# TensorE's order inside the attention loops: transposes of a pair ahead of the product with V

## The chip, the cores and the metric

One Trainium2 chip, one core. The metric is the device time of the whole program in microseconds (us). The engines are TensorE (PE; its weight loads are shown apart as PEld), VectorE (DVE), ScalarE (ACT), GpSimd (POOL) and SyncE (SP).

## What is computed

Two models of depth two run one after the other on 256 tokens of width 1024. The second also carries 256 context tokens in its first layer. Most of the time goes to plain products with streamed weights. The change touches only the three attention loops:

```python
# first model, layer 1 ("nsa"): 16 heads, 256 queries; p over 256 keys for two branches (selected, window), plus a compressed branch
s = einsum(qc, k) - slope * distance ;  p = masked_softmax(s) ;  o = einsum(p, v)
# second model, layer 0 (512 tokens) and layer 1 (256 latent queries, 512 keys)
"gqa": s = einsum(q, k) ;          p = softmax(s) ; o = einsum(p, v)
"na":  s = einsum(q, k) + bias ;   p = softmax(s) ; o = einsum(p, v)
```

The output is the normalised state of the 256 tokens.

## The kernel before, in words

The program is written engine by engine; each engine runs its own list in order and waits on semaphores where it needs another's result. The order of work around the change is written out by hand in four functions of the same name, `softmax`, one each for PE (L717), ACT (L1143) and DVE (L1507), over the list that `attention_jobs` (L243) gives. No planner sets it.

A job is one head and 128 queries. Jobs go in pairs (two heads that share the rows of a tile), numbered u = 0, 1, 2 and so on. The first loop, called **nsa** here, has 16 pairs; even pairs have q = 0 (128 keys in each of two branches) and odd pairs q = 1 (256 keys in each). The second loop, **layer 0**, has 32 pairs, 16 of kind gqa and then 16 of kind na; within each kind u mod 4 is 0 or 1 for queries over 512 keys and 2 or 3 for queries over 256 keys. The third loop, **layer 1**, has 16 pairs, 8 gqa and then 8 na, all over 512 keys.

What is done to pair u, step by step:

- PE computes the **scores** of both heads into a double bank of PSUM (L734 to L740; two double banks, `score_pairs`), and waits first for ACT's exponentials of pair u-2 in that bank (L727). Its matmuls are recorded by the helper `mm`, L579.
- DVE adds the causal term (L1524, nsa) or the position bias (L1531, na, 256 of its keys), and takes the row **maximum** (L1535; for gqa a factor at L1538).
- ACT takes the **exponentials** into `s_p`, one of four buffers per head (L1166), recorded at L1020, with the row sums read by an extra instruction each.
- DVE takes the reciprocal of the sums (L1545; L1550 multiplies the gates in, nsa) and scales the rows: the **normalisation** (L1555), which signals `prob_ready`. DVE does this for pair v-1 after the maximum of pair v.
- PE makes the **transposes** (L781) into `turn_pair`, banks 6 and 7 of PSUM, of which there is one copy: 8 matmuls of 128x128 in most pairs, 4 where the pair has half the keys. They wait for `prob_ready` of the pair and for ACT's copy of pair u-1, and signal `turned_full`.
- ACT **copies** the transposed rows to SBUF (L1156), into one half of a buffer `pT` that holds two pairs, and signals `turned_ready`.
- PE makes the **product with V** of two pairs at once, in every even turn, and signals `o_full`; ACT copies its result out (L1174).

PE's loop runs over turns v. Turn v has the scores of pair v; in even turns from v = 4 the product with V of pairs v-4 and v-3; and from v = 2 the transposes of pair v-2. In ACT's loop, turn v has the copy of pair v-2, then the exponentials of pair v, and in odd turns the copy of a product.

Two waits in an even turn v matter. The product with V waits for `turned_ready` of pair v-3, and so do the transposes of pair v-2 (both ask for v-2 copies in the loop). And ACT's copy of pair v-2 overwrites the half of `pT` from which the product of this same turn reads pair v-4; it waits for it:

```python
act.wait_ge(turned_full, base // 2 + u + 1)                    # L1152
if u >= 2:
    act.wait_ge(o_full, base // 4 + (u - 2) // 2 + 1)          # L1154
```

For even u = v-2 that is the product of turn v; for odd u it is the product of the turn before.

Of the kernel before, what the change touches and what calls it, by code (L numbers as in the profile page):

```python
# [31 lines left out]
P = 128  # L32
# [237 lines left out]
def turned_blocks(kind, q):  # L270

    if kind == "nsa":
        return [2 * br + b for br in range(2) for b in range(q + 1)]
    return list(range(len(key_blocks(kind, q))))
# [14 lines left out]
def program(nc, wstream, params_in, consts_in, rpb_in, c_in, x_in, out):  # L289
    ctx = ExitStack()  # L290
    with ctx:
# [280 lines left out]
        def _(pe):  # L572
# [144 lines left out]
            def softmax(layer=None):  # L717

                jobs = attention_jobs(layer)
                pairs = len(jobs) // 2  # L720
                base = jobs_done.base
                for v in range(pairs + 3):
                    if v < pairs:
                        kind, t, _, q = jobs[2 * v]
                        qs = slice(q * P, (q + 1) * P)
                        if v >= 2:
                            pe.wait_ge(prob_exp, base + 2 * v - 2)  # L727
                        for p in range(2):
                            rows_ = slice(DH * p, DH * p + DH)
                            bank = score_pairs[v % 2][:, p, :]  # L730
                            if kind == "nsa":

                                nk = (q + 1) * P
                                ins = mm(bank.rearrange("p (b k) -> p b k", b=2)[:, :, 0:nk], n_q[rows_, t, qs],  # L734
                                         n_k[rows_, :, t // GROUP, 0:nk], start=True, stop=True)
                            else:
                                a = 0 if q < 2 else S
                                key = a_nak[rows_, t, a:S2] if kind == "na" else a_gk[rows_, a:S2]
                                qq = (a_naq if kind == "na" else a_gq)[rows_, t, qs]
                                ins = mm(bank[:, 0:S2 - a], qq, key, start=True, stop=True)  # L740
                        ins.then_inc(score_full, 1)
                    if v >= 4 and v % 2 == 0:

                        i = 2 * (v - 4)
                        kind, t, _, q = jobs[i]
                        out_ = (base + i) // 4
                        if out_ >= 2:
                            pe.wait_ge(o_free, out_ - 1)
                        pe.wait_ge(turned_ready, (base + i) // 2 + 2)
                        pT = n_pT if kind == "nsa" else a_pT  # L750
                        terms = []
                        for p in range(2):
                            head = head_of(kind, t, p)
                            if kind == "nsa":
                                g = head // GROUP
                                mine = [(n_vz[:, head, :], n_pcT[:, :, g, :], 0)]
                                for b in range(2):
                                    for br in range(2):
                                        k = (br * 2 + b) * P
                                        mine.append((n_v[:, b, (br * KV + g) * DH:(br * KV + g + 1) * DH], pT[:, 2 * b + p::2, k:k + P], b))  # L760
                            else:
                                mine = []
                                for n, b in enumerate(key_blocks(kind, q)):
                                    val = a_nav[:, b, head * DH:(head + 1) * DH] if kind == "na" else a_gv[:, b, p * DH:(p + 1) * DH]
                                    mine.append((val, pT[:, p::2, n * P:(n + 1) * P], 0))
                            terms.append(mine)
                        last = len(terms[0]) - 1
                        for n in range(last + 1):
                            for p in range(2):
                                val, pr, first = terms[p][n]  # L770
                                ins = mm(out_banks[out_ % 2][DH * p:DH * p + DH, first * P:S], val, pr, start=n == 0, stop=n == last)
                        ins.then_inc(o_full, 1)
                    if 2 <= v < pairs + 2:
                        u = v - 2
                        kind, t, _, q = jobs[2 * u]
                        pe.wait_ge(prob_ready, base + 2 * u + 2)
                        if u >= 1:
                            pe.wait_ge(turned_ready, base // 2 + u)
                        for p in range(2):
                            for b in turned_blocks(kind, q):  # L780
                                ins = nc.tensor.transpose(turn_pair[:, p, b * P:(b + 1) * P], s_p[:, (2 * u + p) % 4, b * P:(b + 1) * P], ident)  # L781
                        ins.then_inc(turned_full, 1)
                jobs_done.base += len(jobs)

            pe.wait_ge(ones_ready, 1)
# [1187 lines left out]
```

## Time and profile before

| | before |
|---|---|
| median of 3 runs | 2247.96 us (2245.68 to 2248.45) |
| profiled execution, its own time | 2248.55 us |
| its span | 2246.7 us |
| PE busy | 2103.2 us (94%) |
| DVE busy | 1514.9 us (67%) |
| ACT busy | 875.6 us (39%) |
| granted TensorE clock, mean | 0.97 |

In the rows below times are in us from the start of the span. A matmul's end is modelled, so that successive groups of matmuls overlap by some hundredths; the distance from start to start is what counts. A granted clock of 1.00 is TensorE at 2.4 GHz and 0.50 is 1.2 GHz. In square brackets stands how long the engine was idle before the row, and which engine's instruction ended that.

### The profile page before, as it was taken

Reading aid. Unit: us, or ns where it says so; the run is one execution under the profiler, and the core shown is the slowest. Engines: PE = TensorE matmul, PEld = TensorE weight load, DVE = VectorE, ACT = ScalarE, POOL = GpSimd, SP = SyncE. Lnnn points to the kernel's source line nnn. Section 1 sums busy time; section 2 is a strip of 40 time slices with the busy share of each in tenths; the row PEclk is TensorE's granted clock in tenths of the full one; section 3 lists DMA queues with packets and bytes.
Section 4 is the critical chain, followed back from the end, with each engine's and each line's share of the span. In section 5 each row is a group of like instructions: output and inputs, shape, how many; then the busy total and the mean of one; then the engine's idle time right before and its main releaser. Section 6 shows DMA issues by size and latency. Waiting matters only on the chain.

```text
span 2246.7 us, 33659 instructions
## 1 busy us (share of the span) xinstructions
PE 2103.2 (94%) x12858; PEld 1791.8 (80%) x12858; DVE 1514.9 (67%) x2859; ACT 875.6 (39%) x1376; POOL 249.5 (11%) x231
## 2 busy tenths in 40 slices
PE   7899999879999799889899989999997998999998
PEld 6789999748999588646567568888886865998998
DVE  7658898395888669776698863383276966355554
ACT  4634444273444432475211242212214336435443
POOL 0003321003330010000000002201211000001220
PEclk9999999889999899999999999999998999999999
DMA  6345465404556322103455422252243310344552
GB/s 234 121 175 190 179 248 209 149 1 165 188 179 260 134 95 76 57 1 132 152 213 207 170 111 94 93 193 107 94 169 123 131 57 20 151 176 162 186 187 78
DMA packets 46987, 318.09 MB, mean 142 GB/s; under 512 B 5008, under 2 KB 8080, under 8 KB 9488
## 3 DMA queue, kind: packets, MB, share of 16 engines
q1 hardware_dynamic: 45568, 309.58, 37.4%
q0 software_dynamic: 1296, 6.82, 0.8%
q8 instruction: 84, 1.38, 0.2%
q14 instruction: 39, 0.32, 0.0%
HBM read 315.33 MB, written 1.05 MB: 141 GB/s over the span
## 4 chain that ended last, share of the span: by engine, by line
PE 72%; DVE 17%; ACT 5%; issue 3%; DMA 2%; DVEq 0%; ACTq 0%; SPq 0%
PE ps L579 68%; DVE ps L1373 4%; DVE w_lo L1353 4%; ACT arena L1020 3%; DMA ring<-wstream 2%; PE ps L781 2%; PE ps L627 1%; DVE arena L1337 1%; DVE small L1535 1%; DVE rs L1319 1%; DVE arena L1555 1%; DVE h_lo L1347 1%; ACT w_hi L1020 1%; ACT L1020 1%; DVE ps L1524 1%
## 5 line engine op out<-in xcount | busy, mean ns | idle before, releaser
L579 PE MATMUL ps<-h_hi,w_hi 128*128 128x256 f32 (+1 forms) x2616 | 849.2, 325 | 48.7 <-DVE h_lo L1347 30.7
L579 PE MATMUL ps<-h_lo,w_hi 128*128 128x256 f32 (+1 forms) x2616 | 834.9, 319 | 0.0
L579 PE MATMUL ps<-h_hi,w_lo 128*128 128x256 f32 (+1 forms) x2616 | 833.8, 319 | 0.0
L1353 DVE TENSOR_TENSOR w_lo<-ring,w_hi 128x1024 fp32r<-128x1024 f32 x433 | 545.2, 1267 | 356.5 <-ACT w_hi L1020 355.7
L1020 ACT ACTIVATE w_hi<-ring 128x1024 fp32r<-128x1024 f32 x433 | 452.3, 1055 | 582.0 <-PE ps L579 476.6
L579 PEld LDWEIGHTS ps<-h_hi,w_hi 128*128 128x128 f32 x2616 | 503.0, 192 | 98.7 <-issue 42.9
L579 PEld LDWEIGHTS ps<-h_lo,w_hi 128*128 128x128 f32 x2616 | 504.6, 193 | 33.2 <-issue 1.2
L579 PEld LDWEIGHTS ps<-h_hi,w_lo 128*128 128x128 f32 x2616 | 504.5, 193 | 33.0
L1020 ACT ACTIVATE arena<-ps 128x512 f32<-128x512 f32 (+2 forms) x246 | 140.9, 575 | 461.1 <-PE ps L579 415.1
L1373 DVE SCALAR_TENSOR_TENSOR ps<-ring,arena 128x512 f32<-128x512 f32 x384 | 250.8, 725 | 0.0
L579 PE MATMUL ps<-arena,ring 128*128 128x256 f32 (+2 forms) x840 | 217.6, 420 | 20.6 <-DMA ring<-wstream 7.8
L579 PE MATMUL ps<-hid_hi,w_hi 128*128 128x256 f32 (+1 forms) x736 | 224.6, 305 | 0.9 <-DVE w_lo L1353 0.9
L579 PE MATMUL ps<-hid_lo,w_hi 128*128 128x256 f32 (+1 forms) x736 | 224.3, 305 | 0.0
L579 PE MATMUL ps<-hid_hi,w_lo 128*128 128x256 f32 (+1 forms) x736 | 224.3, 305 | 0.0
L579 PEld LDWEIGHTS ps<-arena,ring 128*128 128x128 f32 x840 | 150.9, 193 | 84.2 <-issue 54.5
L520 POOL CAST hid_hi<-arena 128x256 f32 (+3 forms) x92 | 82.5, 897 | 1024.8 <-DVE arena L1471 1024.8
L579 PE MATMUL ps<-arena 128*64 128x256 f32 (+4 forms) x800 | 129.5, 449 | 28.4 <-ACT arena L1020 24.7
L579 PEld LDWEIGHTS ps<-hid_hi,w_hi 128*128 128x128 f32 x736 | 138.4, 188 | 9.4 <-issue 1.2
L579 PEld LDWEIGHTS ps<-hid_lo,w_hi 128*128 128x128 f32 x736 | 138.1, 188 | 8.2
L579 PEld LDWEIGHTS ps<-hid_hi,w_lo 128*128 128x128 f32 x736 | 138.0, 188 | 8.1
L1687 DVE SCALAR_TENSOR_TENSOR arena<-arena,prm 128x512 f32<-128x512 f32 (+1 forms) x240 | 129.9, 613 | 0.4
L579 PEld LDWEIGHTS ps<-arena 128*64 128x64 f32 (+1 forms) x800 | 63.4, 174 | 70.4 <-issue 37.4
(153 smaller groups left out, 1673.3 us busy)
## 6 DMA issues: line engine op xcount, KB each, us to landing
ring<-wstream SPq DMA_DIRECT2D x290, 1024.0 KB, 4.8
arena<-c_in POOLq DMA_DIRECT2D x7, 512.0 KB, 4.5
arena<-rpb POOLq DMA_DIRECT2D x2, 1536.0 KB, 8.2
x<-x_in SPq DMA_DIRECT2D x2, 1024.0 KB, 12.1
out<-arena SPq DMA_DIRECT2D x8, 128.0 KB, 2.0
cst<-consts SPq DMA_DIRECT2D x1, 928.0 KB, 11.9
prm<-params SPq DMA_DIRECT2D x1, 580.0 KB, 10.6
ring<-wstream SPq DMA_DIRECT2D x1, 512.0 KB, 3.5
```

What stands on the lines that cost most here:

```text
L520: nc.gpsimd.tensor_copy(hi, products[:, e, 0:N]).then_inc(pool_step, 1)
L579: ins = nc.tensor.matmul(*a, **k)
L627: ins = nc.tensor.matmul(psO[:, 0:N], ones[:], sq[:, k % 4, 0:N], start=k == 0, stop=k == KD - 1)
L781: ins = nc.tensor.transpose(turn_pair[:, p, b * P:(b + 1) * P], s_p[:, (2 * u + p) % 4, b * P:(b + 1) * P], ident)
L1020: return nc.scalar.activation(o, i, f, **k)
L1319: link(V.reciprocal(rs[:, 0:N], rs[:, 0:N]))
L1337: V.scalar_tensor_tensor(out=scaled[:, n % 8, :], in0=x[:, k, c], scalar=gain(k, s), in1=rs[:, c], op0=ALU.mult, op1=ALU.mult).then_inc(sc ...
L1347: ins = V.scalar_tensor_tensor(out=h_lo[:, k, c], in0=t, scalar=bias(k, s), in1=hi, op0=ALU.add, op1=ALU.subtract)
L1353: V.tensor_tensor(w_lo[:, job % SPLITS, :], raw_job(job), w_hi[:, job % SPLITS, :].bitcast(F32), ALU.subtract).then_inc(weights_ready, 1)
L1373: V.scalar_tensor_tensor(out=ps[4 + p][:], in0=w, scalar=1.0, in1=c[s][:, p * S2:(p + 1) * S2], op0=ALU.mult, op1=ALU.mult, accum_out=mod_ ...
L1524: ins = V.scalar_tensor_tensor(out=sc, in0=c, scalar=slope, in1=sc, op0=ALU.mult, op1=ALU.add)
L1687: return V.scalar_tensor_tensor(out=cy[:, c, 0:ns, :], in0=a_u3[:, c, 0:ns, bass.ds(j, S)], scalar=w, in1=cy[:, c, 0:ns, :], op0=ALU.mult, ...
```

## The change

In PE's loop the block that makes the transposes of pair v-2 stands ahead of the block that makes the product with V, where it stood behind it. Both blocks keep their instructions, waits and signals. Nothing else changes; odd turns have no product with V, and turns 2 and 3 and those from pairs + 2 on have only one of the two blocks, so the order of their work is the same.

```diff
                         ins.then_inc(score_full, 1)
+                    if 2 <= v < pairs + 2:
+                        u = v - 2
+                        kind, t, _, q = jobs[2 * u]
+                        pe.wait_ge(prob_ready, base + 2 * u + 2)
+                        if u >= 1:
+                            pe.wait_ge(turned_ready, base // 2 + u)
+                        for p in range(2):
+                            for b in turned_blocks(kind, q):
+                                ins = nc.tensor.transpose(turn_pair[:, p, b * P:(b + 1) * P], s_p[:, (2 * u + p) % 4, b * P:(b + 1) * P], ident)
+                        ins.then_inc(turned_full, 1)
                     if v >= 4 and v % 2 == 0:
...
                         ins.then_inc(o_full, 1)
-                    if 2 <= v < pairs + 2:
-                        u = v - 2
-                        kind, t, _, q = jobs[2 * u]
-                        pe.wait_ge(prob_ready, base + 2 * u + 2)
-                        if u >= 1:
-                            pe.wait_ge(turned_ready, base // 2 + u)
-                        for p in range(2):
-                            for b in turned_blocks(kind, q):
-                                ins = nc.tensor.transpose(turn_pair[:, p, b * P:(b + 1) * P], s_p[:, (2 * u + p) % 4, b * P:(b + 1) * P], ident)
-                        ins.then_inc(turned_full, 1)
                 jobs_done.base += len(jobs)
```

## Rows read from the trace of the kernel before

**Rows 1.** The page, busy time, share of the span and instructions of PE.
```profile
PE 2103.2 (94%) x12858; PEld 1791.8 (80%) x12858; DVE 1514.9 (67%) x2859; ACT 875.6 (39%) x1376; POOL 249.5 (11%) x231
```
**Rows 2.** Busy time by stretch, the three loops: PE, PEld, DVE, ACT, POOL, PEclk, DMA.
```profile
449.00:511.00 62.00, 48.73 (x320) 29.52 (x320) 51.35 (x145) 41.90 (x152) 0.00 (x0) 0.86 0.00 1
932.00:1030.00 98.00, 80.68 (x514) 46.44 (x515) 65.92 (x160) 71.26 (x179) 0.15 (x1) 0.97 0.00 1
1839.00:1900.00 61.00, 50.80 (x320) 28.33 (x320) 42.36 (x88) 42.06 (x89) 0.00 (x0) 0.97 0.00 1
```
**Rows 3.** Chain of waits and list of waits (total, times, longest), 445 to 511 us.
```profile
by line: DVE arena L1555 21.4%; DVE ps L1524 21.3%; DVE small L1535 21.1%; PE ps L579 12.9%; ACT arena L1020 5.1%; DVE small L1550 3.7%; PE ps L781 3.4%; PE ps L893 3.0%; issue 2.4%; DVE small L1545 2.2%; DVE arena L1636 1.1%; DVE arena L16
...
PE ps L781 <- DVE arena L1555: 5.6, 7, 1.2
```
**Rows 4.** Timeline of the nsa loop, turn 10 and the start of turn 11.
```profile
479.13 1.29 DVE L1524 SCALAR_TENSOR_TENSOR ps<-cst,ps 128x512 f32<-128x512 f32 x2
480.29 0.70 PE L579 MATMUL ps<-arena 64*128 64x256 f32 x4
480.40 1.02 ACT L1020 ACTIVATE arena<-ps 128x1024 f32<-128x1024 f32 x1 [0.76 <-PE ps L781]
481.57 1.95 PE L579 MATMUL ps<-arena 128*64 128x256 f32 x20 [0.57 <-ACT arena L1020]
481.99 0.87 DVE L1555 TENSOR_SCALAR arena<-arena,small 128x128 f32<-128x128 f32 x4
483.45 0.65 PE L781 MATMUL ps<-cst,arena 128*128 128x128 f32 x4
484.04 1.13 PE L579 MATMUL ps<-arena 64*128 64x512 f32 x4
485.63 1.29 DVE L1524 SCALAR_TENSOR_TENSOR ps<-cst,ps 128x512 f32<-128x512 f32 x2
```
**Rows 5.** Timeline of the nsa loop, turns 16 to 18.
```profile
501.51 0.88 DVE L1555 TENSOR_SCALAR arena<-arena,small 128x128 f32<-128x128 f32 x4
...
504.80 1.09 PE L781 MATMUL ps<-cst,arena 128*128 128x128 f32 x8 [1.18 <-DVE arena L1555]
507.09 3.50 PE L579 MATMUL ps<-arena 128*64 128x256 f32 x20 [1.21 <-ACT arena L1020]
```
**Rows 6.** Timeline of layer 0, kind gqa: turn 12 (first row) and turn 14.
```profile
966.17 0.62 DVE L1555 TENSOR_SCALAR arena<-arena,small 128x256 f32<-128x256 f32 x2
...
972.43 0.88 DVE L1555 TENSOR_SCALAR arena<-arena,small 128x512 f32<-128x512 f32 x2
...
973.65 1.09 PE L781 MATMUL ps<-cst,arena 128*128 128x128 f32 x8
```
**Rows 7.** Timeline of layer 0, kind na: turn 22.
```profile
995.27 0.88 DVE L1555 TENSOR_SCALAR arena<-arena,small 128x512 f32<-128x512 f32 x2
...
996.21 1.09 PE L781 MATMUL ps<-cst,arena 128*128 128x128 f32 x8 [0.43 <-DVE arena L1555]
```
**Rows 8.** Timeline of layer 1: turn 6 (gqa), turn 10 (na).
```profile
1857.76 3.01 PE L579 MATMUL ps<-arena 64*128 64x512 f32 x20 [0.36 <-ACT arena L1020]
1857.94 0.88 DVE L1555 TENSOR_SCALAR arena<-arena,small 128x512 f32<-128x512 f32 x2
...
1870.91 3.01 PE L579 MATMUL ps<-arena 64*128 64x512 f32 x20 [0.18 <-ACT arena L1020]
1871.69 0.88 DVE L1555 TENSOR_SCALAR arena<-arena,small 128x512 f32<-128x512 f32 x2
...
1873.85 1.09 PE L781 MATMUL ps<-cst,arena 128*128 128x128 f32 x8
1874.87 1.13 PE L579 MATMUL ps<-arena 64*128 64x512 f32 x4
```
**Rows 9.** Busy time by stretch, as rows 2: ends of nsa and of layer 1.
```profile
503.40:506.90 3.50, 1.31 (x11) 0.86 (x8) 1.30 (x5) 1.60 (x4) 0.00 (x0) 1.00 0.00 0
...
1893.20:1897.80 4.60, 2.21 (x18) 1.72 (x17) 0.49 (x2) 2.17 (x3) 0.00 (x0) 1.00 0.00 0
```

## The prediction, made before the changed kernel ran

> **What bounds the kernel now.** The page first: PE is busy for 94% of the span, so that most of the program is a stream of matmuls the change does not touch [rows 1]. The stretches of the three attention loops come next [rows 2]. They are different: the nsa loop has PE busy for 48.7 of 62 us and DVE for 51.4, layer 0 has PE 80.7 of 98 and layer 1 50.8 of 61. No engine is full in any of them for the whole stretch, hence the time is set by a cycle of waits that goes round once in two turns, and I read that cycle from the timelines. DMA moves nothing in them (share 0.00), and the weights' queue on SP waits for no instruction that is moved, so no transfer enters the argument. What follows a loop is bound by PE and can only start when the loop has ended; a loop that ends later moves all that follows by as much.
>
> In nsa the chain goes for over 60% through DVE's L1555, L1524 and L1535, one after another, and PE waited 7 times for the normalisation before transposes, 5.6 us in all [rows 3]. In turn 10 PE makes the scores from 480.29, waits 0.57 us for ACT's copy of pair 7 (begun at 480.40), runs 20 matmuls of the product from 481.57, transposes from 483.45, and has turn 11's scores from 484.04 [rows 4]. Put simply, in an even turn the product waits for the copy, and the transposes for the copy and the normalisation. The normalisation of turn 10 began at 481.99 and took 0.87: it ended at 482.86, under the product. That is the cover which the change takes away.
>
> **The change, part by part.** No instruction is added or removed, nothing goes to another engine, no DMA is moved. In each even turn that has both blocks two things change.
>
> (a) The transposes now stand directly behind the scores. They cannot start before the normalisation, so PE idles where it ran the product. Behind the waiting transposes are queued the product and then the next turn's scores.
>
> (b) ACT's copy of the transposed rows can't profit. It waits for the product of the same turn too (L1154), since it overwrites what that product reads. Today it starts when transposes end; afterwards it starts when the product ends. Call T the moment at which both blocks of an even turn are done. Today and afterwards the copy and the next scores start from T. So the price of the change is how much later T is, turn by turn, if everything else keeps its distance from T.
>
> The steps, from rows. The hand-over from DVE's end to PE's transposes is 0.06 (996.21 less 995.27 and 0.88) [rows 7]. Four transposes advance PE by 0.59 (484.04 less 483.45) [rows 4], eight by 1.02 (1874.87 less 1873.85) [rows 8]. The product advances it by 1.88 in nsa (483.45 less 481.57) [rows 4]. In layer 1 scores and product together take 2.94 (1873.85 less 1870.91), of which the scores are some 1.08 and the product 1.86 [rows 8].
>
> *nsa, 7 turns (4 to 16).* New T in turn 10, with the normalisation's end where it is: 482.86 + 0.06 + 0.59 + 1.88 = 485.39, against 484.04 today, 1.35 later [rows 4]. DVE's next step on those scores, the bias add, starts at the earliest 1.17 behind T (1.13 of scores and a hand-over): 486.56. Today DVE starts it at 485.63, 1.59 behind T, since it is busy until then. So 0.42 of the 1.35 disappears in that slack, and 0.93 per two turns is left. The new cycle closes: bias add to the end of the normalisation is 482.86 less 479.13, or 3.73; 3.73 + 2.53 + 1.17 = 7.43 against 6.50 (485.63 less 479.13). Six such turns make 5.6 us. In the seventh, turn 16, the normalisation ends at 501.51 + 0.88 = 502.39, the product at 504.92, the copy follows by 0.10 and the last transposes follow the start of that copy (half the size of the one of 1.02 us, 0.60) by some 0.74; they start at 505.76, against 504.80 today [rows 5]: 0.96. Together 6.5 us.
>
> *Layer 0, 15 turns (4 to 32).* In 8 of them (v a multiple of 4) the pair to be transposed has half the keys, and its normalisation is done at 966.17 + 0.62 = 966.79, before the scores of that turn, which began at 965.99 and last over 1 us, are finished [rows 6]. The copy ends last there for both blocks and the swap costs nothing; what hides the swap is the copy, and if that were 0.3 us shorter, nothing would be lost either. In 3 gqa turns (6, 10, 14) the normalisation ends at 972.43 + 0.88 = 973.31. Transposes at 973.37, eight of them to 974.39, and then the product. It has 8 matmuls, half of those that take 1.86 in layer 1 [rows 8], so 0.93 and a hand-over, say 1.0: T is 975.39 against 973.65 + 1.02 = 974.67 today, 0.7 each [rows 6]. In 4 na turns (18, 22, 26, 30) PE already waits 0.43 for DVE behind the product, so the whole product of 1.0 comes on top [rows 7]. There DVE's chain hangs on T of the turn before and moves with it. Sum 3 x 0.7 + 4 x 1.0 = 6.1 us.
>
> *Layer 1, 7 turns (4 to 16).* In the 3 gqa turns the normalisation ends at 1858.82, and PE, with the scores done at 1858.84, would start at 1858.88: 0.04 each [rows 8]. In na DVE has the bias add in front of its maximum, so the normalisation is later: 1871.69 + 0.88 = 1872.57. Transposes from 1872.63 to 1873.65, product to 1875.51, against 1874.87: 0.64 [rows 8]. Turn 16 is taken like it. Sum 0.1 + 4 x 0.64 = 2.7 us.
>
> **Sum:** 6.5 + 6.1 + 2.7 = 15.3 us, onto the profiled execution's 2248.55: 2263.9, rounded to 2264. The median of the runs stands 0.6 below that execution, so by the median it would be 2263.3. Outside the loops I cost the edit at nothing. Waits that PE has in odd turns (for ACT's copy, and in nsa for DVE, 5.6 us in 7 times [rows 3]) all hang on T or get shorter, since DVE gains time there; nothing in rows lets them grow.
>
> **Unknown costs, from both sides.** The clock is the one thing that rows of today do not show for the new pattern. From 503.40 to 506.90 PE was busy for 1.31 of 3.50 us, in waits of 1.18 and 1.21, and then the product ran at 3.50 instead of 1.95: the granted clock had fallen from 2.4 to 1.2 GHz [rows 4, 5, 9]. At layer 1's end PE was busy for 2.21 of 4.60 us and the clock stayed at 1.00 [rows 9]. The new nsa turns have one idle stretch of about 2 us, longer than these waits, but with PE busier on either side. (From the scores' end, 480.99, to 482.92 it is 1.9 with today's times [rows 4]; normalisation moves 0.9 away, and the rest is a matter of how far the odd turn's wait for DVE, some 0.8 [rows 3], shrinks.) A fall costs, for as long as it lasts, 1.55 on a product (3.50 for 1.95) and in the same ratio 0.5 on four transposes and 0.9 on the scores that DVE waits for, 3 us per two turns. Lower end nothing, upper end all seven nsa turns, 21 us. I take nothing, by the nearest row: the new turns have one long wait each and a product and scores on either side, like layer 1's end, which kept the clock, where nsa's end had two waits with only transposes between. A gain is not excluded: a product which starts right behind transposes has its weights loaded already, and no wait of its own to come back from. That hand-over is 0.15 at most (481.57 less 480.40 and 1.02) [rows 4].
>
> **Rivals.**
>
> *The clock falls in nsa, and perhaps in layer 0's na turns.* For it: nsa's end today [rows 5, 9]. Against it: layer 1's end [rows 9]. Two of the nsa turns at half clock give 6 us more, 2270; all seven 2285. I give this rival 0.22. The Trainium skill (TensorE: Matmul & The Clock Gate, Part 4: PE-mode transpose) says transposes don't count as work for the clock in the way matmuls do. By that rule the new order invites the fall, since it puts transposes right behind the idle stretch, and the time would be this rival's 2270 and not 2264. The trace agrees at nsa's end, where between the products of turns 16 and 18 only transposes ran and the clock fell [rows 5, 9]; at layer 1's end the stretch that holds the transposes of turns 16 and 17 left it up [rows 9], so the trace does not decide.
>
> *DVE draws level.* If the normalisation, freed of other lateness, came 0.4 us sooner in nsa and na turns than the fixed distance from T, each of 14 turns would lose less: about 8 to 10 us in all, 2257. For it: DVE has idle time in layer 0 (65.9 of 98). Against: what it waits for there are scores, which follow T. 0.10.
>
> *Not slower: one wait instead of two.* If the normalisation reached PE before the copy in every even turn, as it does in 8 of the 29, the swap would cost nothing and save one hand-over of up to 0.15 per turn, 29 x 0.15 = 4 us: 2244. It decides at the end of the even turn's scores; the normalisation stands 0.04 to 2 us behind that point in 21 turns [rows 4, 6, 7, 8]. 0.05.
>
> *The change doesn't do what it says.* PE's list is executed in the order written and no other engine's list sets the order of the two blocks; 2248, 0.02.
>
> **How the numbers follow.** Forecast 0.61, clock 0.22, DVE 0.10, not slower 0.05, no change 0.02. A difference of 0.2%, 4.5 us, is about what a measurement of this kernel can tell from none. Slower by over 0.2% holds the first three, 0.93; within it 0.04; faster 0.03. The range reaches down to 2257, the DVE case, and up to 2271, two or so turns at half clock. The predicted time is the sum, 2264.
>
> **What would show it.** Right: in the nsa loop pairs of turns 7.4 us apart instead of 6.5, transposes of even turns idle before them until DVE's L1555, the product directly behind, ACT's copy behind the product; layer 0's na turns 1.0 longer, layer 1's gqa turns unchanged. Wrong: even turns of the old length, or a copy by ACT that starts before the product has ended, or a granted clock of 0.50 inside a loop beyond its first turns.

## The result, and the profile of the changed kernel

The changed kernel took 2275.12 us (median of 4 runs, 2274.14 to 2275.74) against 2248.2 (median of 4, 2245.68 to 2250.75) for the kernel before: a ratio of 1.0119, 95% interval 1.0102 to 1.0137. It is slower, as forecast, but by 27 us where 15 were forecast, and outside the range of 2257 to 2271. The profiled execution took 2274.14 us, its span is 2272.3; against the profiled execution of before that is 25.6 us more.

The first part of the page of the changed kernel: busy time, share and instructions. The work is the same, count for count [rows 1]. PE is busy for 9.5 us longer, its weight loads for 3.1, and the other engines for 0.3 at most; as PE makes the same matmuls, some of them must have run slower.

```profile
PE 2112.7 (93%) x12858; PEld 1794.9 (79%) x12858; DVE 1515.2 (67%) x2859; ACT 875.6 (39%) x1376; POOL 249.5 (11%) x231
```

To see where the 25.6 us are I cut both timelines at the first scores matmul of each loop and at the first matmul behind it, and at the last matmul of the program (9.2 us follow it in both), in us:

| stretch | before | changed | difference |
|---|---|---|---|
| up to nsa | 449.55 | 452.57 | 3.0 |
| nsa loop | 61.52 | 71.11 | 9.6 |
| nsa to layer 0 | 421.36 | 420.07 | -1.3 |
| layer 0 loop | 97.17 | 106.42 | 9.25 |
| layer 0 to layer 1 | 809.43 | 808.89 | -0.5 |
| layer 1 loop | 61.21 | 66.80 | 5.6 |
| from there to the last matmul | 337.29 | 337.26 | 0.0 |

24.4 us are in the three loops, 1.2 outside them. The stretches outside vary from execution to execution of any kernel here: the one up to nsa has lain between 449.6 and 453.9, the one up to layer 1 between 805.5 and 813.8. In the loops the price was forecast as 6.5, 6.1 and 2.7.

The timeline of the nsa loop of the changed kernel, PE alone, from turn 6 on (x24 is the product and the next turn's scores in one row):

```profile
473.78 0.66 PE L750 MATMUL ps<-cst,arena 128*128 128x128 f32 x4 [2.06 <-DVE arena L1555]
474.36 4.69 PE L579 MATMUL ps<-arena 128*64 128x256 f32 x24
...
482.90 0.66 PE L750 MATMUL ps<-cst,arena 128*128 128x128 f32 x4 [2.05 <-DVE arena L1555]
483.49 3.01 PE L579 MATMUL ps<-arena 128*64 128x256 f32 x24
486.43 1.09 PE L750 MATMUL ps<-cst,arena 128*128 128x128 f32 x8
...
490.35 0.66 PE L750 MATMUL ps<-cst,arena 128*128 128x128 f32 x4 [2.05 <-DVE arena L1555]
490.93 4.65 PE L579 MATMUL ps<-arena 128*64 128x256 f32 x24
```

Two things are to be seen. First the pattern: an even turn's transposes wait some 2.05 us for the normalisation, the product stands directly behind, and from 482.90 to 490.35 two turns take 7.45 us, where they took 6.50 and were forecast at 7.43 [rows 4]. Second, two rows that break it: the same 24 matmuls take 4.69 and 4.65 us instead of 3.01, and those pairs of turns take 9.12 and 9.08. The views of the same stretch for DVE and ACT show where T's delay goes:

```profile
480.11 1.02 ACT L1020 ACTIVATE arena<-ps 128x1024 f32<-128x1024 f32 x1
...
481.97 0.87 DVE L1555 TENSOR_SCALAR arena<-arena,small 128x128 f32<-128x128 f32 x4
...
485.55 0.60 ACT L1020 ACTIVATE arena<-ps 128x512 f32<-128x512 f32 x1 [1.65 <-PE ps L579]
...
486.55 1.29 DVE L1524 SCALAR_TENSOR_TENSOR ps<-cst,ps 128x512 f32<-128x512 f32 x2 [0.85 <-PE ps L579]
```

ACT's copy (485.55) waits for the product, DVE's bias add (486.55) for the scores behind it, 0.85 us idle: DVE, which was the chain in this loop [rows 3], now stands still for PE. The list of waits of the changed kernel, 445 to 517 us (total, times, longest), has them beside PE's:

```profile
PE ps L750 <- DVE arena L1555: 15.8, 8, 2.8
...
DVE ps L1524 <- PE ps L579: 10.3, 9, 2.5
```

The timeline of layer 0, kind na, PE: turns 22 and 26. The wait is 1.38 us where it was 0.43 [rows 7]; in the second pair the product of 12 matmuls takes 2.93 instead of 1.72.

```profile
1011.09 1.09 PE L750 MATMUL ps<-cst,arena 128*128 128x128 f32 x8 [1.38 <-DVE arena L1555]
1012.11 1.72 PE L579 MATMUL ps<-arena 128*64 128x256 f32 x12
...
1023.42 1.46 PE L750 MATMUL ps<-cst,arena 128*128 128x128 f32 x8 [1.38 <-DVE arena L1555]
1024.81 2.93 PE L579 MATMUL ps<-arena 128*64 128x256 f32 x12
```

The timeline of layer 1's end, PE: an na turn, turn 16, and the last two products.

```profile
1901.06 1.09 PE L750 MATMUL ps<-cst,arena 128*128 128x128 f32 x8 [0.53 <-DVE arena L1555]
...
1915.34 1.09 PE L750 MATMUL ps<-cst,arena 128*128 128x128 f32 x8 [1.84 <-DVE arena L1555]
1916.37 1.95 PE L579 MATMUL ps<-arena 128*64 128x256 f32 x16
...
1921.86 3.53 PE L579 MATMUL ps<-arena 128*64 128x256 f32 x16 [1.21 <-ACT arena L1020]
```

What the slow rows have in common is in the busy time by stretch of the changed kernel (columns as in rows 2; the third from the end is the granted clock):

```profile
474.50:477.90 3.40, 3.40 (x20) 1.96 (x18) 2.00 (x7) 0.26 (x1) 0.00 (x0) 0.51 0.00 0
491.50:494.90 3.40, 3.40 (x20) 1.97 (x18) 1.58 (x7) 0.71 (x2) 0.00 (x0) 0.50 0.00 0
1024.00:1027.40 3.40, 3.40 (x17) 1.76 (x15) 0.94 (x3) 0.63 (x2) 0.00 (x0) 0.50 0.00 0
1037.60:1041.00 3.40, 3.40 (x17) 1.69 (x15) 0.93 (x3) 0.69 (x2) 0.00 (x0) 0.51 0.00 0
1921.70:1925.10 3.40, 3.24 (x16) 1.91 (x16) 0.00 (x0) 0.29 (x2) 0.00 (x0) 0.50 0.02 5
```

Five stretches at 1.2 GHz, each just behind a wait of PE for DVE or ACT, in places where the kernel before had 2.4. They cost 1.65 us each in nsa (9.12 or 9.08 less 7.45), some 1.25 each in layer 0 (the first 13.59, from 1023.42 to 1037.01, less 12.33, from 1011.09), and 1.6 in layer 1 (3.53 less 1.95): 7.4 us. A fall in nsa's last turns stands in both kernels (3.4 us from 506.9 before, from 515.4 now) and cancels.

One more difference of the clock is easily missed, in the first turns of layer 1. The scores of turn 3, PE's timeline, before (first row) and in the changed kernel:

```profile
1848.39 1.13 PE L579 MATMUL ps<-arena 64*128 64x512 f32 x4
1868.62 2.04 PE L579 MATMUL ps<-arena 64*128 64x512 f32 x4
```

Half clock lasted 3.4 us there before (from 1844.9) and 6.8 now (from 1863.7). It is not the swap's doing alone, if at all: e2 and e8 below keep layer 1's old order and have the 6.8 too, and turn 5's transposes begin 17.96 and 17.81 us into their loop, against 17.30 before and 18.36 in the changed kernel. So some 0.6 us of layer 1's 5.6 belong to that stretch.

Of the 24.4 us all this leaves 6.3 (nsa), 6.7 (layer 0) and 3.4 (layer 1), 16.4 in all, for waits, and 8.0 for the clock.

### The profile page after: what moved, and what is told of

The parts are those of the page before. It is cut to its first block, busy times and chain, and to the rows that moved or that the text cites. A ratio compares the mean times of both kernels' runs of the same rounds, so it can differ in the third digit from the quotient of the medians.

```text
span 2272.3 us, 33659 instructions
## 1 busy us (share of the span) xinstructions
PE 2112.7 (93%) x12858; PEld 1794.9 (79%) x12858; DVE 1515.2 (67%) x2859; ACT 875.6 (39%) x1376; POOL 249.5 (11%) x231
## 3 DMA queue, kind: packets, MB, share of 16 engines
q8 instruction: 84, 1.38, 0.2%
HBM read 315.33 MB, written 1.05 MB: 139 GB/s over the span
## 4 chain that ended last, share of the span: by engine, by line
PE 73%; DVE 18%; ACT 4%; issue 3%; DMA 2%; DVEq 0%; ACTq 0%; SPq 0%
PE ps L579 69%; DVE ps L1373 4%; DVE w_lo L1353 4%; DMA ring<-wstream 2%; ACT arena L1020 2%; PE ps L750 2%; PE ps L627 1%; DVE small L1535 1%; DVE arena L1337 1%; DVE rs L1319 1%; DVE arena L1555 1%; DVE h_lo L1347 1%; ACT w_hi L1020 1%; ACT L1020 1%; DVE arena L1687 1%
## 5 line engine op out<-in xcount | busy, mean ns | idle before, releaser
L579 PE MATMUL ps<-arena 128*64 128x256 f32 (+4 forms) x800 | 136.3, 473 | 21.4 <-ACT arena L1020 18.4
L522 POOL TENSOR_TENSOR hid_lo<-arena,hid_hi 128x256 f32 (+3 forms) x92 | 114.9, 1249 | 15.1 <-POOL hid_hi L520 14.8
```

What stands on the lines that cost most here:

```text
L522: nc.gpsimd.tensor_tensor(lo, products[:, e, 0:N], hi.bitcast(F32), ALU.subtract).then_inc(pool_written, 1)
L579: ins = nc.tensor.matmul(*a, **k)
```

## The experiments

The theory: 16 to 17 us are waits (the queue on PE holds the product and the next scores behind the normalisation), and some 7 us the clock, which falls because of them. The rivals: the copy by ACT, which now waits for its own turn's product, is the price; the clock is noise that comes and goes without the change; the cost is in the swap itself and is the same in every turn. All kernels but two (e9, e10) compute all of the reference. `product_of` and `turn_of` are the two blocks of the diff, as functions; "before" and "changed" say which order the turns not named have.

**e1, e2, e3: the swap in one loop at a time.**

```diff
-                    product_of(v)
-                    turn_of(v)
+                    if layer is None:        # e1; layer == 0 in e2, layer == 1 in e3
+                        turn_of(v)
+                        product_of(v)
+                    else:
+                        product_of(v)
+                        turn_of(v)
```

> Transposes first in the nsa loop only. Theory (PE idles for the normalisation, 0.93 us a pair of turns, and the longer idle stretches make the granted clock fall, some 1.6 us a time): 6.5 us of waits and about 3 of clock, so 9 to 10 us slower than before; pairs of turns 7.4 apart, one or two of them 9.1. Rival (the clock would have fallen anyway and the excess over the forecast comes from elsewhere): 6.5 us slower and no 0.50 inside the loop.

> Transposes first in layer 0's loop only. Theory: 3 x 0.75 + 4 x 1.05 = 6.4 us of waits, and in the na turns, where PE now idles for 1.4 us at a stretch, up to 2.6 us of lower clock: 7 to 9 us slower. Rival (no clock effect): 6.4. Nsa and layer 1 as in the kernel before.

> Transposes first in layer 1's loop only. Theory: gqa turns 0.1 longer, na turns 0.65, turn 16 one of 0.7, then 3 us, plus up to 2 us if the clock falls at the end: 3 to 5 us slower. The three loops alone should add up to what the whole change costs, 27 us less what is noise outside; if one part changed another, they would not.

Measured: e1 2260.07 us, ratio 1.0048 (1.0035 to 1.0060); e2 2260.57, 1.0043 (1.0030 to 1.0056); e3 2253.84, 1.0019 (1.0011 to 1.0028); before in the same session 2250.56. The sum of the three differences is 9.5 + 10.0 + 3.3 = 22.8 us, and of the ratios' excess 0.0110 against 0.0119. The swapped loop took 71.40, 107.00 and 66.65 us, as in the changed kernel (71.11, 106.42, 66.80). So the three loops add up, each pays for itself, and nothing else of the program is touched. e1 and e2 each had two stretches of clock 0.50 inside the swapped loop, beyond its first turns and before its last ones, at other moments than the changed kernel had; in the loops that kept the old order none lay there, save one at layer 1's end in e2 (1908.1 to 1911.5). That one shows that layer 1's end falls without the swap as well, now and then. Nsa's end is no different: it kept the clock in e2, e3 and e4, in the old order, where the kernel before had lost it [rows 5]. e2 came out a little above its expected 7 to 9 us, e1 and e3 within theirs.

**e4: the swap where the normalisation is done early.** Layer 0 alone, turns that are a multiple of 4.

```diff
-                    product_of(v)
-                    turn_of(v)
+                    if layer == 0 and v % 4 == 0:
+                        turn_of(v)
+                        product_of(v)
+                    else:
+                        product_of(v)
+                        turn_of(v)
```

> Transposes first only in the 8 turns of layer 0 whose normalisation is ready before the scores end (v a multiple of 4). Theory: nothing, within 1 us, since the copy by ACT ends last for both blocks and T stays. Rival (the order itself costs or gains a hand-over per turn): 8 x 0.15 = 1.2 us either way.

Measured: 2250.71 us, ratio 1.0000 (0.9991 to 1.0009), layer 0's loop 97.28 against 97.17, as expected. The swap itself has no price: it costs what its wait is late by. The hand-over that it might have saved doesn't show either.

**e5, e6: work for PE in the long wait.** The changed kernel; ahead of the wait of the transposes, in nsa's turns 4 to 14 and layer 0's turns 18, 22, 26 and 30, PE makes products with the identity (5 of 128x256, e5) or transposes of the identity (7, e6) into a PSUM bank that is free.

```diff
+                        if v >= 4 and v % 2 == 0 and v < pairs and (layer is None or layer == 0 and v % 4 == 2 and jobs[2 * v][0] == "na"):
+                            o_ = (base + 2 * (v - 4)) // 4
+                            if o_ >= 2:
+                                pe.wait_ge(o_free, o_ - 1)
+                            for _ in range(5):          # e6: range(7)
+                                nc.tensor.matmul(out_banks[o_ % 2][:, 0:S], ident, cst[:, 0:S], start=True, stop=True)
+                                # e6: nc.tensor.transpose(out_banks[o_ % 2][:, 0:P], ident, ident)
                         turn_of(v)
                         product_of(v)
```

> The changed kernel, with 5 products of the identity (128x128 by 128x256) in front of the wait for the normalisation, in nsa's turns 4 to 14 and layer 0's turns 18, 22, 26, 30; they are written into the bank that the next product overwrites. They add about 1.1 us of PE work a time inside a wait of 1.4 to 2.05 us. Theory (the clock falls because PE idles there): the granted clock stays at 1.00 in both loops, pairs of turns stay at 7.45 and 12.3, and the kernel gets 4 to 6 us faster than the changed one, about 2270. Rival (the falls have nothing to do with that wait): unchanged at 2275, or slower.

> The same with 7 transposes of the identity instead of 5 products, about 0.9 us of PE work a time. If transposes count for the clock as products do: as the run with products, about 2270. If they don't count (the Trainium skill, TensorE: Matmul & The Clock Gate, Part 4: PE-mode transpose, says they count differently): the falls stay, and the time is the changed kernel's 2275.

Measured: e6 2271.54 us, ratio 1.0084 (1.0071 to 1.0097); e5 2279.62, 1.0120 (1.0105 to 1.0134). PE's timeline of e6, nsa and layer 0's na turns (L784 are the transposes of the pair, L793 the added ones, L1571 the normalisation):

```profile
474.11 0.66 PE L784 MATMUL ps<-cst,arena 128*128 128x128 f32 x4 [1.14 <-DVE arena L1571]
...
479.44 0.98 PE L793 MATMUL ps<-cst 128*128 128x128 f32 x7
481.56 0.66 PE L784 MATMUL ps<-cst,arena 128*128 128x128 f32 x4 [1.14 <-DVE arena L1571]
...
1012.39 0.98 PE L793 MATMUL ps<-cst 128*128 128x128 f32 x7
1013.84 1.09 PE L784 MATMUL ps<-cst,arena 128*128 128x128 f32 x8 [0.46 <-DVE arena L1571]
1014.86 1.72 PE L579 MATMUL ps<-arena 128*64 128x256 f32 x12
```

The wait is cut from 2.05 to 1.14 us, the turns' times stay (7.45 a pair, 481.56 less 474.11), and from 466.67 to 503.90 not one pair took longer: no stretch of 0.50 lay in the turns with added work. Layer 0's loop took 103.05 against 106.42; 2.5 of the 3.4 us are the two falls, and the rest is that half clock in its first turns, where nothing was added, lasted 3.4 us and not 6.8. In nsa's turns 4 to 14 the clock fell twice each in the changed kernel, e1 and e7, and never in e5, e6 and e12; in layer 0's turns 18 to 30 twice each in the changed kernel and e2, and never in e5, e6 and e12 (in e5 it fell once behind them, from 1044.9, where nothing was added). So it is the wait that brings these falls on. nsa's loop still took 70.03, as the clock fell in its last turns, where nothing was added (512.8 to 523.0). And e5 missed its expected 2270, for a reason of its own. PE's timeline of e5, the same two places:

```profile
480.33 2.43 PE L793 MATMUL ps<-cst 128*128 128x256 f32 x10
482.60 0.60 PE L784 MATMUL ps<-cst,arena 128*128 128x128 f32 x4
...
1023.92 2.43 PE L793 MATMUL ps<-cst 128*128 128x256 f32 x10
1026.19 1.04 PE L784 MATMUL ps<-cst,arena 128*128 128x128 f32 x8
```

Five products advance PE by 2.27 us (482.60 less 480.33), twice what I had put. That is a little more than nsa's wait of 2.05 (pairs of turns 7.53 apart), and the 1.38 us wait in layer 0 could not hide them: its loop took 108.62. The clock stayed at 1.00 in the turns with added work, in both loops, but as a measure in time of the clock's part e5 is void.

**e7: the copy freed of its own product.** The swap in nsa alone, with two buffers for the transposed rows, so that ACT's copy waits for the product of the pair before, long done.

```diff
-        n_pT = part(14112, 4, S2)
+        n_pT = (part(7264, 4, S2), part(14112, 4, S2))
...
-                        if u >= 2:
-                            act.wait_ge(o_full, base // 4 + (u - 2) // 2 + 1)
+                        old = 4 if kind == "nsa" else 2
+                        if u >= old:
+                            act.wait_ge(o_full, base // 4 + (u - old) // 2 + 1)
```

> Transposes first in nsa only, and pT for nsa with room for four pairs, so that ACT's copy no longer waits for the product of its own turn. Theory (nsa is late because the next scores are queued behind wait, transposes and product): the copy starts right behind the transposes, 1.9 us earlier, and the pairs of turns stay at 7.4; as slow as the same loop without the wider buffer, 9 to 11 us slower than before. Rival (the copy behind the product is what costs): the loop gets back to 6.5 and the kernel to within 2 us of before.

Measured: 2259.64 us, ratio 1.0037 (1.0025 to 1.0048), nsa's loop 70.53 (e1: 71.40). The timeline of e7 (L784 transposes, L1030 ACT, L1566 normalisation):

```profile
483.94 0.66 PE L784 MATMUL ps<-cst,arena 128*128 128x128 f32 x4 [2.20 <-DVE arena L1566]
...
484.53 3.01 PE L579 MATMUL ps<-arena 128*64 128x256 f32 x24
484.54 0.88 ACT L1030 ACTIVATE arena<-ps 128x256 f32<-128x256 f32 x2
...
487.59 1.29 DVE L1535 SCALAR_TENSOR_TENSOR ps<-cst,ps 128x512 f32<-128x512 f32 x2 [0.85 <-PE ps L579]
...
491.39 0.66 PE L784 MATMUL ps<-cst,arena 128*128 128x128 f32 x4 [2.19 <-DVE arena L1566]
```

The copy now starts right behind the transposes, at 484.54, where in the changed kernel it stands 2.06 us behind them (485.55 less 483.49), and two turns still take 7.45 (491.39 less 483.94). DVE waits the same 0.85 for scores. The copy was not the price in nsa; there the first rival falls. In layers 0 and 1 it was not tested.

**e8: the scores freed too.** As e7, but in nsa PE makes the transposes, then the odd turn's scores, and only then the product.

```diff
                     if layer is None:
+                        if v % 2:
+                            product_of(v - 1)
                         turn_of(v)
-                        product_of(v)
+                        if v == pairs + 2:
+                            product_of(v)
```

> As the run before, but nsa's product stands one turn later, behind the next scores: transposes first, then the odd turn's scores, then the product. Theory: with only the transposes (0.6 us) between the normalisation and the next scores DVE is the bound again, pairs of turns 6.5 apart, and the kernel is within 2 us of before (a little over 0 at the loop's end). Rival (waiting for the normalisation ahead of the product costs in itself, wherever the scores stand): 5 us or more slower than before.

Measured: 2254.84 us (one of the 12 runs took 5334.36 us, for no cause that I know), ratio 1.0015 (1.0006 to 1.0024), between the 2 us that I had expected and the rival's 5; nsa's loop took 64.52, with one stretch of 0.50 in it (483.5 to 486.9, behind waits of 0.58 and 1.07 with four transposes between them). The timeline of e8 (L784 transposes, L1033 ACT, L1569 normalisation; x24 is the odd turn's scores and the product):

```profile
496.39 0.66 PE L784 MATMUL ps<-cst,arena 128*128 128x128 f32 x4 [0.58 <-DVE arena L1569]
...
498.12 3.01 PE L579 MATMUL ps<-arena 64*128 64x512 f32 x24 [1.07 <-ACT arena L1033]
...
501.06 1.09 PE L784 MATMUL ps<-cst,arena 128*128 128x128 f32 x8
```

Half of the loss is gone, and the long wait for DVE with it (0.58 instead of 2.05), but the pairs are 6.97 apart rather than 6.50 (7.45 in the changed kernel). Now PE's scores wait 1.07 for ACT, and the product, 20 matmuls at 498.12, stands in front of the next transposes. So the scores queued behind the product are about half of nsa's price, and in both places tried for the product in the changed order something is queued behind it. The other half is put down to that by the timeline alone; no run takes it away.

**e9, e10: the normalisation cut short.** L1555 scales only 16 columns of each block; the rest of the probabilities stays unscaled, in both. e9 is the kernel before with that, e10 the changed one.

```diff
-                                ins = V.tensor_scalar(o[:, br, :], o[:, br, :], s_rec[:, c:c + 1], None, ALU.mult)
+                                ins = V.tensor_scalar(o[:, br, 0:16], o[:, br, 0:16], s_rec[:, c:c + 1], None, ALU.mult)
```

> The kernel before, with the normalisation (L1555) cut to the first 16 columns of each block; the rest of the rows is left unscaled. A control for the next run. Layers 0 and 1 are not bound by the normalisation there, so they stay within 2 us of 97 and 61; nsa, which DVE bounds, gets about 10 us shorter.

> The changed kernel with the same cut, which leaves the rest of the rows unscaled: the wait that the change exposes gets about 0.6 us shorter a turn (0.88 to some 0.25). Theory (PE's wait for the normalisation is what costs): against the control, layer 0 costs 2 to 4 us instead of 9, layer 1 at most 2 instead of 5.6, and the granted clock stays up in both. Rival (the order costs by itself, by the copy behind the product or by hand-overs): the cost against the control stays at 9 and 5.6.

Measured: e9 2243.97 us, ratio 0.9969 (0.9957 to 0.9982); e10 2259.52, 1.0042 (1.0028 to 1.0057). The loops took 58.03, 95.19, 63.64 in e9 and 67.98, 100.28, 62.92 in e10. In e9 nsa got 3.5 us shorter where I had expected 10, and layer 1, with 2.4 us more instead of at most 2, lost the clock at its end. PE's timeline of e10, layer 0's na turn:

```profile
1004.75 1.09 PE L750 MATMUL ps<-cst,arena 128*128 128x128 f32 x8 [0.86 <-DVE arena L1555]
1005.77 1.72 PE L579 MATMUL ps<-arena 128*64 128x256 f32 x12
```

The wait shrinks from 1.38 to 0.86 by the 0.5 us that the normalisation is shorter, and four turns take 11.82 instead of 12.33. But four turns of e9 also shrank, from 11.28 to 10.77: as DVE is the chain there in either order, the product's 1.05 us come on top in either length. Only the gqa turns got cheaper, from 0.77 to 0.26 (11.22 less 10.96). Layer 0's loss therefore fell only to 5.1 us (4 x 1.05 and 3 x 0.26 are 5.0), where I had expected 2 to 4. Layer 1's is at most 0.9 (62.92 against 63.64, of which the clock took some 1.6 in e9), and e10 has no clock of 0.50 in either layer beyond the first turns: shorter waits, no fall. In nsa, where the wait was still 1.82, the clock fell once inside the loop (494.3 to 497.7). There the swap costs even more than before: pairs are 7.22 apart in e10 and 5.94 in e9 (489.72 less 477.85 makes two), since a shorter normalisation helps the old order as well. A shorter chain on DVE doesn't repair the new order.

**e11: the old order, with work for PE where its clock falls.** Seven identity products in turn 1 of layers 0 and 1, and seven identity transposes each ahead of nsa's last transposes and last product.

```diff
+                    if v == 1 and layer is not None:
+                        for _ in range(7):
+                            nc.tensor.matmul(out_banks[0][:, 0:S], ident, cst[:, 0:S], start=True, stop=True)
+                    if layer is None and v in (pairs + 1, pairs + 2):
+                        pe.wait_ge(o_free, pairs // 2 - 2)
+                        for _ in range(7):
+                            nc.tensor.transpose(out_banks[1][:, 0:P], ident, ident)
                     if v >= 4 and v % 2 == 0:
```

> The kernel before, in its own order, with idle stretches filled: 7 products of the identity in turn 1 of layers 0 and 1 (PE waits 3.66 us there today and the clock falls), and 7 transposes of the identity in front of the last transposes and the last product of nsa (waits of 1.18 and 1.21). They are written into banks that a later product overwrites. If idle PE is what lowers the clock: the clock stays at 1.00 at these places and the loops start 1 to 3 us sooner each, 2 to 5 us faster than before. Rival (the exponentials that end those waits bound the first turns): nothing, within 1 us.

Measured: 2245.05 us against 2250.69, ratio 0.9970 (0.9958 to 0.9982), faster than before and a little beyond the 2 to 5 us expected. PE's timeline at nsa's end (L748 added work, L788 the pair's transposes), to be read beside rows 5:

```profile
506.98 0.99 PE L748 MATMUL ps<-cst 128*128 128x128 f32 x7
508.30 1.09 PE L788 MATMUL ps<-cst,arena 128*128 128x128 f32 x8 [0.33 <-DVE arena L1562]
509.23 0.93 PE L748 MATMUL ps<-cst 128*128 128x128 f32 x7
510.60 1.62 PE L579 MATMUL ps<-arena 128*64 128x256 f32 x14 [0.44 <-ACT arena L1027]
```

The product that took 3.50 us at half clock [rows 5] runs at full clock, and the granted clock is 1.00 in these stretches of e11:

```profile
506.00:510.00 4.00, 3.67 (x36) 3.08 (x32) 1.49 (x6) 2.10 (x7) 0.00 (x0) 1.00 0.00 0
936.00:942.00 6.00, 5.14 (x30) 3.80 (x29) 4.12 (x12) 4.69 (x10) 0.00 (x0) 1.00 0.00 0
1843.00:1848.00 5.00, 4.19 (x24) 2.32 (x24) 4.36 (x9) 4.22 (x10) 0.00 (x0) 1.00 0.00 0
```

The loops took 59.90, 95.60 and 61.15 against 61.52, 97.17 and 61.21, 3.25 us less. How much of that the added work did differs by place. Layer 0's 1.6 us are its doing: the kernel before, e1, e3, e7 and e8, which keep the old order there, took 97.2 to 97.4, all with 6.8 us of half clock in the first turns. In layer 1 e11 is likewise the only kernel without half clock in the first turns; what that gained was lost again as the clock fell at the loop's end (1894.7 to 1898.1). Nsa's 1.6 us can't be put down to it, as e2, e3 and e4 took 59.9 to 60.0 with nothing added. The profiled execution was 1.4 us faster than that of before (2247.19 against 2248.55), and where the rest of the 5.6 us between the medians lies no trace shows.

**e12: the changed kernel with all its long waits filled.** As e6, and also the last turns of nsa (14, 5 and 7 transposes) and of layer 1 (9, 5 and 7).

```diff
+                        n_ = 0
+                        if v >= 4 and v % 2 == 0 and v < pairs and (layer is None or layer == 0 and v % 4 == 2 and jobs[2 * v][0] == "na"):
+                            n_ = 7
+                        if v >= pairs and layer != 0:
+                            n_ = (14 if layer is None else 9, 5, 7)[v - pairs]
```

> The changed kernel with transposes of the identity in all of its long waits: 7 a time in nsa's turns 4 to 14 and layer 0's na turns, and 14, 5, 7 in nsa's and 9, 5, 7 in layer 1's last three turns. With the clock up everywhere in the loops, what is left is the wait for the normalisation alone: by the forecast's steps, with 0.6 more for layer 1's turn 4, 16 us slower than before, 14 to 18, against 27 for the changed kernel. If more than 20 us are left, there is a cost besides waits and clock.

Measured: 2270.53 us against 2250.84, ratio 1.0086 (1.0071 to 1.0102). Busy time by stretch of e12:

```profile
463.00:519.00 56.00, 47.59 (x368) 32.00 (x367) 40.43 (x117) 35.22 (x126) 1.12 (x2) 1.00 0.02 6
989.00:1045.00 56.00, 46.04 (x306) 27.53 (x305) 34.00 (x78) 36.67 (x93) 1.09 (x2) 1.00 0.04 11
```

The clock is 1.00 through nsa's swapped turns and layer 0's na turns. The loops took 66.52, 103.09 and 65.26. A loop of the old order without a fall in its last turns takes 59.9, 97.2 and 61.2 (e3 and e4: 59.90 and 59.93; e1: 97.22 and 61.20), so the differences are 6.6 + 5.9 + 4.1 = 16.6 us. The first turns, where nothing was added, had another clock than those references: half of it for 3.4 us less in layer 0 and for 3.4 us more in layer 1. In layer 0 that is worth 0.9 us (turn 4's transposes begin 12.26 us into the loop here and 13.12 in the changed kernel, which had the 6.8), in layer 1 the 0.6 of above. The waits alone are then 6.6, 6.8 and 3.5, 16.9 us. Nsa's last turns are the best case for the added work: with the swapped order the clock fell there in the changed kernel, e1, e5, e6, e7 and e10, and only here it stayed. The median is 19.7 us over before, beyond the 14 to 18 that I had expected. The profiled execution is 19.4 over, of which 4.4 lie outside the loops (the stretch up to layer 1 took 812.05, and the clock was 0.50 in it from 1176.0 to 1179.4, in work that the change doesn't touch).

## Why the prediction was wrong in size and right in direction

**Nothing is added, and what bounds the loops.** Right. Counts are the same, and 24.4 of 25.6 us lie in the three loops (e1 to e3 add up to 22.8).

**nsa, 6.5 us by waits.** Right: 6.3 from the changed kernel's table, 6.6 from e12, though with some luck: turn 16 cost 1.3 where I had 0.96 and turn 4 0.7 where I had 0.93, which cancels. The closed cycle of 7.43 came out as 7.45. The 0.42 of slack that DVE had before its bias add is used up, and it waits 0.85 instead. The mechanism is the one given in (a): e7 shows that the copy of (b) doesn't count, and e8 that the queued scores are about half.

**Layer 0, 6.1.** Right: 6.7 from the table, 6.8 from e12. The na turns cost 1.05 a piece (12.33 less 11.28) where I had 1.0, the gqa turns 0.77 (11.73 less 10.96) where I had 0.7. The eight turns costed at nothing cost nothing (e4).

**Layer 1, 2.7.** Somewhat mis-sized: 3.4 and 3.5. The na turns were right, 0.66 each for 0.64 (7.14 less 6.48), and so was the last one, turn 16, that I had "taken like" them: its wait was 1.84, but from turn 15's transposes to the loop's end e12 took 11.84 and the kernel before 11.13, 0.7 more. Too small were the gqa turns, of which turn 4 waited 0.43 for DVE and cost 0.4 to 0.55 (18.36 less the 17.96 of e2 or the 17.81 of e8) and the next ones 0.13 each, all put at 0.04.

**The step that failed: "I take nothing", for the clock.** The clock fell twice in nsa, twice in layer 0's na turns and once at layer 1's end, 7.4 us, and half clock lasted longer in layer 1's first turns, 0.6. With the 1.1 by which the waits were more than 15.3, and 1.2 outside the loops, that is the whole distance from 15.3 to 25.6. The reasoning was by the nearest row, layer 1's end with the clock kept [rows 9], and it was the wrong row: the clock fell there in the old order too, in e2, e8, e9 and e11, and stayed in e1, e4 and e7, so one execution that kept it was chance. The row on the other side was chance as well: nsa's end, which fell before, kept the clock in e2, e3 and e4. The bounds (nothing to 21 us) held the 7.4, and a clock of 0.50 inside a loop beyond its first turns was named as a sign of being wrong.

The rival "the clock falls" had the mechanism, at 0.22, and a price for nsa only, and that price was nearly twice too high: 3 us a fall, for transposes, product and scores of two turns, where a fall lasted 3.4 us and cost 1.65. Its 2270 for two falls in nsa would thus have been 2267. That the waits bring the falls on is shown in nsa and layer 0 by e5, e6 and e12, and in layer 0 by e10: less idle time, by added work or by an earlier normalisation, and the clock stays. Layer 1's end lost the clock in four of eight kernels of the old order and in all four of the changed one that had the full wait (the changed kernel, e3, e5, e6), so that its 1.6 us are not shown to be the swap's.

**Whether transposes count.** I had the rule of the Trainium skill that transposes don't count as work for the clock in the way matmuls do (TensorE: Matmul & The Clock Gate, Part 4: PE-mode transpose) speak for the rival. The rival came true, but not by that rule: seven transposes of 0.98 us together kept the clock in nsa and layer 0 (e6, e12), as five products of 2.27 did (e5), and in e12 14, 5 and 7 of them kept it in nsa's last turns, where six kernels of the swapped order lost it. Here the measurement decides against the rule, for fp32 transposes through the identity.

**The other rivals.** "DVE draws level" is out: nsa's pairs took 7.45, and the na turns of layer 0 cost 1.05. "One wait instead of two" is out too: in e4, where it had its best case, the gain was 0.0.

## What to carry to other kernels

On an engine that works its list in order, moving a waiting block forward costs what its wait is late by, for everything queued behind it, even if the sum of work is unchanged; find the block that the slowest engine needs next, and keep the wait behind it. Price the clock together with each wait on PE that grows: where a timeline shows one fall behind a wait, expect some more where new waits are as long, and don't take one execution that kept its clock as evidence. If such a wait can't be removed, a little idle work on PE that fits into it keeps the clock up (e6, e12); the old order with such work was 0.3% faster (e11), of which the trace shows 1.6 us in layer 0 as its doing. And compare a stretch with the same clock on both sides: layer 1's first turns differed by 0.6 us for that reason alone.

## What the hardware showed that I had not expected

A single wait was enough: PE had the clock cut behind waits of 2.05 us in nsa and of 1.38 us in layer 0, though it had run products and scores on either side; not each time, but in two of six and two of four turns. The same matmuls with the wait filled to 1.14 and 0.46 us never lost it (e6, e12). Nor does it take a long wait: in e8 the clock fell behind 0.58 and 1.07 us with four transposes between. Which turn loses it changes from execution to execution (e1 and the changed kernel). Five fp32 products of 128x256 advance PE by 2.27 us, 0.45 each, where seven transposes of 128x128 take 0.98, 0.14 each, both at a granted clock of 1.00.
